# A 64-byte shift of the buffers behind the eps tile in a two-layer transformer trunk on one core

## What is computed

```python
for l in range(2):
    h = h + 0.5 * swiglu(rmsnorm(h, ffn1_norm[l]), ffn1_w_in[l], ffn1_w_out[l])
    u = rmsnorm(h, mix_norm[l])
    q_a, c_kv, iq, ik, iw, z_pool, q_c, gate_pre = split(u @ w_in[l])
    y_a = dsa_attention(...)      # 8 heads, the 128 best keys of an index score, latent keys
    y_b = pool_mixer(...)         # means over windows of 2, 4, 8, 16 tokens
    y_c = mem_attention(...)      # 4 heads over 256 memory tokens
    g = sigmoid(gate_pre)
    merged = g[0]*(y_a @ w_branch_a[l]) + g[1]*(y_b @ w_branch_b[l]) + g[2]*(y_c @ w_branch_c[l])
    h = h + merged @ w_out[l]
    h = h + 0.5 * swiglu(rmsnorm(h, ffn2_norm[l]), ffn2_w_in[l], ffn2_w_out[l])
return rmsnorm(h, final_norm)
```

## The kernel before

| tile | address | past a 128-byte line |
|---|---|---|
| h, u1H, u1L, raw, wH, wL | 16512, 32896, 49280, 65664, 73856, 90240 | 0 |
| near_bias, far_bias, cst | 106624, 114816, 114944 | 0 |
| pr | 116640 | 32 |
| rms, ssq, ta, over_d, over_r | 121408 to 128064 | 64 |
| eps (128 bytes) | 128576 | 64 |
| sg, iw, top8 | 128704, 132800, 132928 | 64 |
| nmax, rsum, rinv | 132960, 132992, 133024 | 96, 0, 32 |
| u0H, u0L, hidH, hidL, mem, mem_rms | 133056, 149440, 165824, 190400, 214976, 223168 | 64 |
| yH, yL, gate_a, qc, kc, vc, z, za, iq, q, qlat, probs, ckv, relu, picks1 | 133056 to 227264 | 64 |
| the tiles of the further groups (picks2, picks3, iq_stack, ik_stack, iqH, part, gate_bc) | within the same space | 64 |

## Time and profile before

### The profile page before, as it was taken

One profiled execution on the slowest core, in us unless ns is written; L12 is line 12 of the kernel. 1 busy time (PEld: TensorE's weight loads), 2 busy tenths in 40 slices (PEclk: granted clock), 3 DMA queues, 4 the chain that ended last, 5 costly groups with the idle time before them and its releaser, 6 DMA issues.

```text
span 2244.8 us, 31758 instructions
## 1 busy us (share of the span) xinstructions
PE 2216.6 (99%) x10262; PEld 1805.1 (80%) x10262; DVE 953.5 (42%) x1716; ACT 523.6 (23%) x1013; POOL 1325.7 (59%) x884
## 2 busy tenths in 40 slices
PE   9999999999999999999999999999999999999996
PEld 6888888877788888888888888888778888888885
DVE  5331344578855433023333223536877453321334
ACT  3110112443553210001111101125445432100111
POOL 7666657644436665665766566584444376656653
PEclk9999999999999999999999999999999999999998
DMA  5243223222113222332333332232211132223222
GB/s 183 96 134 107 94 80 118 93 69 68 62 54 107 94 94 86 101 103 76 105 102 121 110 107 94 76 130 78 69 62 66 48 121 95 93 83 105 99 79 76
DMA packets 68219, 209.88 MB, mean 93 GB/s; under 512 B 7536, under 2 KB 10776, under 8 KB 67864
## 3 DMA queue, kind: packets, MB, share of 16 engines
q1 hardware_dynamic: 64128, 203.62, 27.7%
q10 hardware_dynamic: 3992, 5.00, 0.7%
HBM read 206.48 MB, written 3.68 MB: 94 GB/s over the span
## 4 chain that ended last, share of the span: by engine, by line
PE 93%; DVE 4%; issue 1%; ACT 1%; DMA 1%; POOL 0%; DVEq 0%; ACTq 0%; POOLq 0%; SPq 0%
PE bank L608 29%; PE bank L607 28%; PE bank L606 28%; PE obank L859 1%; PE sbank L804 1%; PE tbank L826 1%; DVE picks L1356 1%; DVE top L1354 1%; PE obank L617 0%; PE sbank L796 0%; PE sbank L779 0%; DMA h<-in_xT 0%; PE obank L843 0%; PE sbank L757 0%; PE sbank L810 0%
## 5 line engine op out<-in xcount | busy, mean ns | idle before, releaser
L541 POOL TENSOR_TENSOR wL<-raw,wH 128x1024 fp32r<-128x1024 f32 (+3 forms) x424 | 896.0, 2113 | 35.4
L538 POOL TENSOR_SCALAR wH<-raw 128x1024 fp32r<-128x1024 f32 (+3 forms) x424 | 397.4, 937 | 842.1 <-PE bank L608 820.1
L608 PE MATMUL bank<-u0L,wH 128*128 128x512 f32 x1376 | 542.1, 394 | 0.0
L607 PE MATMUL bank<-u0H,wL 128*128 128x512 f32 x1376 | 539.3, 392 | 0.0
L606 PE MATMUL bank<-u0H,wH 128*128 128x512 f32 x1376 | 536.1, 390 | 0.0
L607 PEld LDWEIGHTS bank<-u0H,wL 128*128 128x128 f32 x1376 | 258.3, 188 | 61.1 <-issue 1.0
L606 PEld LDWEIGHTS bank<-u0H,wH 128*128 128x128 f32 x1376 | 258.3, 188 | 58.4 <-issue 1.0
L608 PEld LDWEIGHTS bank<-u0L,wH 128*128 128x128 f32 x1376 | 258.7, 188 | 51.5
L606 PE MATMUL bank<-u1H,wH 128*128 128x512 f32 x704 | 293.2, 416 | 0.0
L608 PE MATMUL bank<-hidL,wH 128*128 128x512 f32 x704 | 277.4, 394 | 0.0
L607 PE MATMUL bank<-hidH,wL 128*128 128x512 f32 x704 | 276.0, 392 | 0.0
(11 more groups left out here) (189 smaller groups left out, 2177.8 us busy)
## 6 DMA issues: line engine op xcount, KB each, us to landing
raw<-in_wA SPq DMA_DIRECT2D x176, 512.0 KB, 3.2
raw<-in_wM SPq DMA_DIRECT2D x96, 512.0 KB, 3.3
raw<-in_wB SPq DMA_DIRECT2D x64, 384.0 KB, 3.0
raw<-in_wB SPq DMA_DIRECT2D x64, 320.0 KB, 2.9
raw<-in_wR SPq DMA_DIRECT2D x32, 256.0 KB, 2.5
mem<-in_memT SPq DMA_DIRECT2D x2, 1024.0 KB, 6.9
near_bias<-bias_rows ACTq DMA_DIRECT2D x2, 1024.0 KB, 6.4
outT<-gate_a SPq DMA_DIRECT2D x4, 512.0 KB, 2.7
```

Source lines behind the costliest of these rows:

```text
L538: pool.tensor_scalar(wH[:, w, 0:cols], raw[:, slot, 0:cols], 1.0, 0.0, ALU.mult, ALU.add).then_inc(rounded, 1)
L541: pool.tensor_tensor(wL[:, w, 0:cols], raw[:, slot, 0:cols], wH[:, w, 0:cols].bitcast(F32), ALU.subtract).then_inc(split_done, 1)
L607: pe.matmul(dst, b, hi[:, k, :], start=False, stop=False)
L608: mm = pe.matmul(dst, a, lo[:, k, :], start=False, stop=last and i == len(tiles) - 1)
```

## The change

The eps tile gets 48 columns in place of 32, 192 bytes in place of 128. It is filled whole by one memset (L1215). Every tile allocated behind it starts 64 bytes later: sg at 128768, u0H and yH at 133120, hidH and gate_a at 165888, and so on. All of them but three of the four small ones of 32 bytes (nmax 32 past a line, rsum 64, rinv 96) then start on a 128-byte line.

```diff
@@ -251,7 +251,7 @@
         ta = sb("ta", [P, T])
         over_d = sb("over_d", [P, P])
         over_r = sb("over_r", [P, P])
-        eps = sb("eps", [P, LINE // 4])
+        eps = sb("eps", [P, LINE // 4 + LINE // 8])
         sg = sb("sg", [P, 2, T])
         iw = sb("iw", [P, QB, IH])
         top8 = sb("top8", [P, 8])
```

## The result

The changed kernel takes 2270.31 us (median of 6 runs, 2269.99 to 2270.86), the kernel before 2252.34 (6 runs beside it and earlier, 2246.24 to 2254.43). The ratio is 1.0079, 95% interval 1.0067 to 1.0091. The forecast was 2237.9, on the wrong side of the time before. The profiled execution took 2270.56 us. One of the 29 executions of the kernel before took 4520.87 us, twice as long as the others, and counts in no comparison.

What follows compares the result with a forecast made beforehand. TensorE's matmul pace was taken to bound the kernel. Gains of 14.9 (large matmuls), 0.6 (small attention matmuls) and 0.4 (memory values) sum to 15.9 us, taking the median 2253.84 to 2237.9 us; range 2232 to 2249.

Steps and rivals of the forecast that it cites:

- What bounds the kernel: Whole kernel: TensorE, busy 99% of the span, sets the time by its own pace; weights are split well ahead.
- What differs between them: Large matmuls: the 680.0 ns pace against 686.7 was put down to u1's tiles starting on a 128-byte line.
- the zone: Large moving tiles: u0 is slower for lying high in memory, so 64 bytes do nothing; 2253.8 us, chance 0.11.
- slower: Large tiles: k slices on multiples of 2048 meet the weight load, 4.5 ns over the best pace; 2269 us, chance 0.05.
- The 14.9 us of the sum: Large matmuls of u0, hid and y: 2240 triples each gain 6.67 ns by reaching u1's pace.
- The warning that I noted: Memory keys: 256-wide matmuls with moving operand off a line still step at 113.3 ns, half of u1's 226.7.
- The gain of 0.4 us that I put on the memory's values: Memory values, both layers: 96 matmuls come down from 117.8 to 113.3 ns, 4.5 ns each.
- No change: Large matmuls: the place of the tile in memory decides, not its start on a line; 2253.8 us, chance 0.11.
- Part of it: Large matmuls: only long trains or one matmul of three gain, a third to five sixths; 2240 to 2248, chance 0.12.
- The base: Starting time of the forecast: median 2253.84 us of the runs shown, 7.2 above the profiled execution's 2246.63.
- The Trainium skill's lines of 16 bytes: On-chip memory: starts 64 bytes apart both begin a 16-byte line, so large matmuls gain nothing; 2253.8 us.
- The small terms: Attention's small fp32 matmuls taken at 0.6 us of gain; VectorE's picks and the last store at 0.

Runs made afterwards that it cites:

- eps_plus_192: The kernel before with eps larger by 192 bytes; 2232.58 us (median of 6), ratio 0.9925.
- all_plus_64: The kernel before with a 64-byte pad ahead of h and eps larger by 192 bytes, moving weights and activations alike; 2232.47 us (median of 4), ratio 0.9932.
- eps_plus_256: The kernel before with eps larger by 256 bytes; 2249.72 us (one run).
- eps_plus_320: The kernel before with eps larger by 320 bytes; 2269.97 us (one run).
- eps_plus_128: The kernel before with eps larger by 128 bytes; 2275.18 us (one run).
- weights_plus_64: The kernel before with a 64-byte pad between raw and wH and eps larger by 128 bytes; 2280.02 us (one run).
- eps_plus_160: The kernel before with eps larger by 160 bytes; 2275.76 us (one run).
- eps_plus_224: The kernel before with eps larger by 224 bytes; 2275.62 us (one run).

## Why the prediction was wrong, point by point

**What bounds the kernel** held. TensorE's pace is the time: 2176 triples x 10.5 ns make 22.8 of 23.9 us, and VectorE, GpSimd and the transfers did what they did before. With the right pace in it, the sum would have met the difference of the profiled spans.

**The step that failed** is the one under "What differs between them": that u1 is quicker because it starts on a 128-byte line. The trace had one pair at 680.0 ns and three at 686.7, and many attributes part one from three. I took the attribute that the change is about, and listed the zone beside it. What I left out was the pair's distance from the weight tile, though the table of addresses had both numbers, 128 past a multiple of 256 for u1 and the weights. The rival "slower" even names this pair as the quickest there is, as a point against itself. The runs put in its place: 680.0 ns at distance 0 wherever the tiles lay, 697.2 at 128, 700.0 at -64, -32 and +32, and 686.7 or 700.0 at +64. The 14.9 us of the sum are real and were measured, but at another shift: eps larger by 192 gives the span 2230.1, 14.7 under the profiled 2244.8.

**The warning that I noted** was the right one to stop at. The keys of the memory (256-wide, distance +64) stepped at just half of u1's pace, so being off a line cost them nothing. I used it against the zone and the line alike and left both standing. With 256 columns the order of the distances is another: at distance 0 the keys take 5.75 us (372.49 to 378.24 in the kernel with eps larger by 192), 119.8 ns, where +64 gave 113.3, or 117.7 in the layer with the stretch at 700.0. The gain of 0.4 us that I put on the memory's values had the wrong sign too: they went from 117.8 to 118.9 ns.

**The rivals.** "No change" by zone: refuted by the kernel with eps larger by 192, where the same tiles, still high in memory, run at 680.0. "Part of it": nothing of the gain came at this shift, and at distance 0 all of it came, in all the large triples alike. "Slower": its time, 2269, is 1.3 us from the measured 2270.3, and its idea, that the moving stream and the weights beside it can be badly placed to each other, is what the shifted weights show. Its place was wrong: not a multiple of 2048, since 256 past one gives the same 697.2, and its price was 4.5 ns over the best pace where 5.7 was measured. That the time fits so well is luck in part: the price was 1.2 ns a matmul too low, 8 us over 6720, and the median it started from was 7.2 us above the profiled execution. A probability of 0.05 for the one rival that took the weights' address into account was too little, with only a single quick pair to argue from.

**The base** was off by itself. The profiled execution, 7.2 us under the median, was one with 686.7 ns throughout, and the median of the runs shown was at the highest of three levels. That is why the profiled spans differ by 23.9 us and the medians by 18.0. A sum made against the profile's own pace can't be carried to such a median by a difference.

**The Trainium skill's lines of 16 bytes** (SBUF — State Buffer, Specifications (TRN2)), as the prediction read them, would have had no shift by 64 bytes matter. The runs don't bear that reading out: with every start a multiple of 32 bytes, the triple runs from 680.0 to 700.0 ns.

**The small terms.** The small fp32 matmuls of the attention, VectorE's picks and the last store were taken at 0.6 us of gain together. That gain isn't seen: the first layer's combined projection, which holds the small matmuls and the picks, went from 298.5 us (388.19 to 686.67) to 298.7 (393.98 to 692.66).

**Open.** That the moving stream and the loading of the next weights meet in the memory is what the shifts of either suggest. No run took the weight load away from beside the stream, so it isn't shown. Nor is it known why a train has two paces at +64, why the y run takes 699.7 ns a triple at distance 128 where u0 and hid take 697.2, or whether a distance that was not tried is quicker still.

## What to carry to other kernels

Where TensorE is the bound and its matmuls are long and back to back, read the distance between starts for each pair of operand tiles; a difference of one per cent between like stages, with no wait beside it and the same clock, can be a matter of where they lie. Compare addresses in pairs, moving against stationary, before naming a cause, and try four or five paddings: here 192 bytes of padding are worth 0.75%, 256 bytes change nothing, and 64, 128, 160, 224 and 320 cost 0.8 to 1.3%. The version to keep is eps larger by 192 bytes (2232.58 us); its six runs lie within 1.1 us, where those of the kernel before spread over 9.

## What the runs showed of the hardware that I hadn't expected

| moving start less weight start, within 256 | ns a triple, 512 columns | time of the kernel, us |
|---|---|---|
| 0 (eps_plus_192, all_plus_64, u1 elsewhere) | 680.0 | 2232.6, 2232.5 |
| +64 (before; eps_plus_256, one run at 2249.7) | 686.7 or 700.0 by stretch | 2245.7 to 2255.0 |
| 128 (changed kernel, eps_plus_320) | 697.2 (u0, hid), 699.7 (y) | 2270.3, 2270.0 |
| -64 (eps_plus_128; weights_plus_64, all pairs) | 700.0 | 2275.2, 2280.0 |
| -32, +32 (eps_plus_160, eps_plus_224) | 700.0 | 2275.8, 2275.6 |

The distance repeats after 256 bytes: starts 0 and 256 past a multiple of 2048 give the same 697.2. The pace is not always a sum over single matmuls: with one operand in three at distance 128, a train took 686.7 in one half, where only the misplaced one paid, and 700.0 in another, where all three did. And an unchanged program can sit at different levels, about 4 us apart, of which one stretch at 700.0 makes 3.6, with the granted clock at 1.00 in both of the stretches compared.
